# Key-page splits earlier in the sample attention, two memory projections behind the scores, and the last two selections spread over later heads

## The reference, cut to what matters

```
# sample request b: keys = 256 cached + 8 new, the best 66 by an indexer score are kept
sc  = where(key_pos <= q_pos, indexer_scores(qi, iw, ki_all), -inf)
sel = top_k(sc, 66)
p   = softmax(q . k[sel] * HEAD_DIM**-0.5);  o = p . v[sel]          # 8 heads of 64

# prompt, in blocks of 128 queries (i = 0..7): keys 0..128*(i+1)-1, the best 256 are kept
sc  = where(key_pos <= q_pos, indexer_scores(qi, iw, ki), -inf)
sel = top_k(sc, 256)                                                # blocks i >= 2 have more than 256
o   = softmax(q . k[sel] * HEAD_DIM**-0.5) . v[sel]                 # per head

# memory: mk, mv = split(rms_norm(mem) @ w_kv), 256 rows x 2048 columns
```

## Time and profile before

| | before |
|---|---|
| three executions | 1844.61, 1849.56, 1849.82 us (median 1849.56) |
| the profiled execution | 1846.91 us, span 1845.1 us |
| mean granted TensorE clock | 0.96 |
| busy: PE | 1707.6 us (93%) |
| busy: VectorE (DVE) | 1114.9 us (60%) |
| busy: ScalarE (ACT) | 811.0 us (44%) |
| busy: GpSimd (POOL) | 733.7 us (40%) |
| the chain that ended last | PE 71%, DVE 15%, ACT 6%, issue 4%, POOL 2%, DMA 2% |
| sample attention | about 445 to 562 us of the span |
| prompt's attention | about 562 to 735 us |

### The profile page before, as it was taken

One profiled execution on the slowest core, in us unless ns is written; L12 is line 12 of the kernel. 1 busy time (PEld: TensorE's weight loads), 2 busy tenths in 40 slices (PEclk: granted clock), 3 DMA queues, 4 the chain that ended last, 5 costly groups with the idle time before them and its releaser, 6 DMA issues.

```text
span 1845.1 us, 33734 instructions
## 1 busy us (share of the span) xinstructions
PE 1707.6 (93%) x13725; PEld 1187.0 (64%) x13803; DVE 1114.9 (60%) x1902; ACT 811.0 (44%) x1476; POOL 733.7 (40%) x704
## 2 busy tenths in 40 slices
PE   6999999996776899989887997999999999999998
PEld 3544445444444655545577544888888888899898
DVE  5856656787797764456655238888788787300000
ACT  5455688655435764432456226435444444110100
POOL 3232365987341200320023426666666666411200
PEclk9999999998797999999988998999999999999999
DMA  7031112023522110301344112121121222321211
GB/s 231 9 109 55 35 45 83 23 81 108 168 90 89 62 38 10 103 1 35 106 154 131 58 52 81 47 70 47 49 68 47 62 54 86 98 95 40 95 38 27
DMA packets 136548, 132.75 MB, mean 72 GB/s; under 512 B 15358, under 2 KB 109630, under 8 KB 136356
## 3 DMA queue, kind: packets, MB, share of 16 engines
q1 hardware_dynamic: 123850, 118.79, 20.7%
q10 hardware_dynamic: 12544, 11.80, 2.0%
HBM read 114.58 MB, written 15.98 MB: 71 GB/s over the span
## 4 chain that ended last, share of the span: by engine, by line
PE 71%; DVE 15%; ACT 6%; issue 4%; POOL 2%; DMA 2%; SPq 0%; ACTq 0%; DVEq 0%; POOLq 0%
PE PS L1558 23%; PE PS L1615 5%; PE PS L1616 5%; PE PS L1617 5%; PE PS L940 4%; PE PS L941 4%; PE PS L942 4%; ACT arena L1631 2%; PE PS L1104 2%; PE PS L1102 2%; PE PS L1103 2%; PE PS L1260 2%; ACT arena L1690 2%; PE PS L1272 1%; POOL arena L2964 1%
## 5 line engine op out<-in xcount | busy, mean ns | idle before, releaser
L1558 PE MATMUL PS<-arena 128*128 128x272 f16 (+1 forms) x3696 | 430.5, 280 | 5.0 <-issue 5.0
L1558 PEld LDWEIGHTS PS<-arena 128*128 128x128 f16 (+1 forms) x3696 | 362.5, 98 | 73.1 <-issue 5.4
L1631 ACT ACTIVATE arena<-PS 128x512 f16<-128x512 f32 (+11 forms) x381 | 189.9, 529 | 235.1 <-PE PS L942 81.3
L1631 ACT ACTIVATE arena<-arena 128x512 f16<-128x512 f32 (+5 forms) x214 | 136.3, 658 | 238.6 <-PE PS L1558 117.1
L368 POOL TENSOR_TENSOR arena<-arena 128x512 bf16<-128x512 f32 (+2 forms) x144 | 161.8, 1158 | 184.1 <-ACT arena L359 183.8
L940 PE MATMUL PS<-arena 128*128 128x512 f16 (+3 forms) x648 | 228.1, 362 | 5.2 <-DVE arena L2597 1.4
L941 PE MATMUL PS<-arena 128*128 128x512 f16 (+3 forms) x648 | 227.5, 361 | 0.0
L1615 PE MATMUL PS<-arena 128*128 128x256 f16 (+1 forms) x792 | 216.0, 273 | 1.4 <-POOL arena L918 1.0
L1617 PE MATMUL PS<-arena 128*128 128x256 bf16 (+1 forms) x792 | 215.9, 273 | 0.0
L1616 PE MATMUL PS<-arena 128*128 128x256 f16 (+1 forms) x792 | 215.9, 273 | 0.0
L942 PE MATMUL PS<-arena 128*128 128x512 bf16 (+2 forms) x608 | 212.0, 359 | 0.0
(11 more groups left out here) (351 smaller groups left out, 3693.6 us busy)
## 6 DMA issues: line engine op xcount, KB each, us to landing
arena<-w_gu SPq DMA_DIRECT2D x44, 512.0 KB, 4.8
arena<-w_down SPq DMA_DIRECT2D x8, 1408.0 KB, 7.8
arena<-w_in SPq DMA_DIRECT2D x8, 1024.0 KB, 5.1
arena<-w_kv_mem SPq DMA_DIRECT2D x8, 1024.0 KB, 7.2
arena<-cache_mem_k SPq DMA_DIRECT2D x32, 256.0 KB, 3.4
arena<-cache_mem_v ACTq DMA_DIRECT2D x28, 256.0 KB, 3.9
arena<-w_in SPq DMA_DIRECT2D x24, 256.0 KB, 3.8
arena<-x_prompt SPq DMA_DIRECT2D x9, 512.0 KB, 6.3
```

Source lines behind the costliest of these rows:

```text
L1558: mm = e.matmul(PS[:, product_bank(f, i) + c, 0:TC], w[:, i, k], s[i][:, q, c, :], start=first, stop=last)
L1631: e.activation(out, in_, ACT.Copy, **kw).then_inc(sem(name), 1)
```

## The change

Four edits, each a move or a condition. No instruction is added or removed.

1. PE: parts 4 and 6 of the memory projection no longer do three groups ahead of the scores; now only the odd parts do, so the wait for a new chunk's weights stands behind the scores.
2. ScalarE: the copies of the next key pages (`page_out`) stand ahead of the weight split, the `sign_step` and the exponential.
3. VectorE: the low parts of the next key pages (`page_lo`) stand right behind the maximum, ahead of the selection's part or `update()` and of the normalisation.
4. VectorE: in the prompt's attention a part of the selection runs only if fewer than four blocks are done, or from head 23 on. Four are done when it begins, so the five open parts (B and C of block 3, A, B and C of block 2) move from heads 0 to 4 to heads 23 to 27.

```diff
+SELECT_FROM = 23
@@ PE, sample attention
-                    if part and part > 2:
+                    if part and part % 2:
                         memory_part(part, 0, 3)
...
                     if part:
-                        memory_part(part, 3 if part > 2 else 0, 6)
+                        memory_part(part, 3 if part % 2 else 0, 6)
@@ ScalarE, step b
                 if b == 5:
                     memory_roots()
+                if b + 1 < DEC_B:
+                    for pg in range(NPG):
+                        page_out(b + 1, pg)
                 if b == 0:
                     e.wait_ge(sem("s2_mm"), NI)
                     B.split_hi(e, 1)
...
                     e.activation(p_s[:, b % 2, :], PS[0:NS, b % 2, 0:PAST + NS], ACT.Exp, bias=sat_st[:, 1, b:b + 1],
                                  scale=ATT_SCALE, accum_out=sat_st[:, 2, b:b + 1]).then_inc(sem("sa_exp"), 1)
-                if b + 1 < DEC_B:
-                    for pg in range(NPG):
-                        page_out(b + 1, pg)
@@ VectorE, step b
                 e.tensor_scalar(sat_st[:, 1, b:b + 1], sat_st[:, 0, b:b + 1], -ATT_SCALE, None, ALU.mult
                                 ).then_inc(sem("sa_nm"), 1)
+                if b + 1 < DEC_B:
+                    page_lo(b + 1, 0)
+                    page_lo(b + 1, 1)
                 if updates[0] == BITS and b < DEC_B - 1:
                     turn(PARTS_SAMPLE[0])
                 update()
...
-                if b + 1 < DEC_B:
-                    page_lo(b + 1, 0)
-                    page_lo(b + 1, 1)
@@ VectorE, prompt's attention, head m
-                turn(PARTS_ATT)
+                if done[0] < 4 or m >= SELECT_FROM:
+                    turn(PARTS_ATT)
```

## The result

| | before | after |
|---|---|---|
| median (lowest to highest) | 1846.74 us (1844.18 to 1849.82, 11 runs) | 1852.04 us (1849.77 to 1853.58, 11 runs) |
| ratio, 95% interval | | 1.0028 (1.0018 to 1.0037) |
| the profiled execution | 1846.91 us | 1853.19 us |

The changed kernel is slower by 5.2 us, between 3.3 and 6.8. The forecast was +2.6 us with "no change" as the likeliest case, so the sign of the sum is right, and it is too small. All ratios here are of fast executions; one of e9's ten, of 4459.63 us, isn't among them.

The account below looks back on a forecast made before the run. PE was taken as busy 93% of the span, with VectorE's list the clock from 480.7 to 500.9 us. The terms +0.7 + 0 - 5.9 + 7.8 = +2.6 us on 1846.91 gave 1849.5 us, range 1840 to 1857.

Parts of the forecast that it names:

- What bounds the kernel: Sample and prompt attention: from 480.7 to 500.9 us VectorE's list is the clock, busy 19.47 of 20.20 us.
- Edits 2 and 3, steps 0 to 2: Sample attention, key pages moved earlier: a later weight load less page work saved on VectorE, +0.7 us.
- The second half of the split of chunk 2 waits for just this transfer: ScalarE, sample attention: this split waits only for the chunk 2 weight load, taken as 1.9 us late.
- The credit of 1.2 us: VectorE, steps 0 to 2: page work no longer stands behind the exponential, -1.2 us.
- the +1.9 for the late split: Steps 0 to 2: the chunk 2 load, and the split that waits for it, come 1.9 us later.
- Edits 2 and 3, steps 3 to 7: Sample attention: VectorE has the same operations in another order and hardly a wait, 0 us.
- Edit 1: PE, sample attention: scores come sooner but nobody needs them, and the projection product is taken out later, 0 us.
- Edit 4, heads 0 to 4: Prompt attention: five selection parts of 9.38 us leave VectorE's list, 3.5 us become waits for PE, -5.9 us.
- Edit 4, heads 23 to 27: Prompt attention: the deferred parts add 5.3 us to the loop and 2.5 us by meeting POOL, +7.8 us.
- Slack takes it all: Rival: deferred parts fall into VectorE's waits and chunk 2's load isn't late, -7.4 us, 1839.5 us; chance 0.18.
- Lock with POOL: Rival: in heads 24 to 26 each two-input VectorE operation waits for a POOL operation, +8.0 us, 1854.9 us; chance 0.16.

Follow-up runs that it names:

- e9: Kernel before with both key-page moves, but ScalarE's copies in step 0 left behind the exponential as before; ratio 1.0010.
- e7: Kernel before with both key-page moves, but in step 2 ScalarE's two page copies stand behind the split of weight chunk 2; ratio 1.0023.
- e5: Kernel before with only ScalarE's page copies moved ahead, VectorE's page subtractions left in place; ratio 1.0035.
- e6: Kernel before with only VectorE's page subtractions moved ahead, ScalarE's page copies left behind the exponential; ratio 1.0039.
- e11: Kernel before with both key-page moves, but VectorE's subtractions behind the search update or selection part, still ahead of the wait for the exponential; ratio 1.0040.
- e1: Kernel before with only the two key-page moves of ScalarE and VectorE, projection order and head loop unchanged; ratio 1.0039.
- e12: Kernel before with only the five selection parts moved, one each ahead of head 0 and at heads 1, 7, 23 and 37; ratio 0.9950.
- e3: Kernel before with only the selection parts moved, out of the first heads to heads 23, 29 and 33 to 35; ratio 0.9990.
- e4: Kernel before with the two key-page moves from step 3 on only, steps 0 to 2 as before; ratio 1.0030.
- e2: Kernel before with only the head-loop gate that defers five selection parts to head 23 and later; ratio 1.0009.

## Why the prediction was wrong in its verdict, point by point

- *What bounds the kernel.* Held. From 480.7 us on VectorE's list is the clock of the stage, and the losses of both kinds reached head 0 in full.
- *Edits 2 and 3, steps 0 to 2: +0.7 us.* **This step failed.** It measured +2.7 against the profiled execution of before, +2.1 against the mean of the six traces with the old code (46.65 us). The first half of its chain came out: split of chunk 1 forecast at 450.6 us (450.27), value pages not before 463.9 (462.50), the load late. What failed was "The second half of the split of chunk 2 waits for just this transfer": it was not asked what `page_out(3)`, moved ahead of that same split, waits for, though the same question had been put for `page_out(1)`. The trace shows 3.26 us of wait for PE there, and behind it PE's 7.00 us of wait for POOL's low halves of chunk 1 and 2.2 us more for the same products at the lower granted clock. The forecast followed these low halves to the value pages and the load, and not to PE. e7 shows that the load was late too, by 2.3 us to the first half, in the range that the text gave and above the 1.9 it took. The credit of 1.2 us for page work that no longer stands behind the exponential appeared in full (1.19); the term mis-sized is the +1.9 for the late split, which measured +3.7. e5 shows that ScalarE's move alone costs about 6 us there, and against it the changed kernel that VectorE's takes 3.5 off; by itself (e6) that one is worth nothing.
- *Edits 2 and 3, steps 3 to 7: 0 us.* **This failed too**, by 2.65 us. The text knew that POOL and VectorE slow one another and took the meetings as a matter of chance, "one or two either way". They are not: the value pages of POOL follow the exponential at a fixed distance, the subtractions push the scan back by 1.2 us in every step, and three of four scans meet POOL in the same way. e11 shows it.
- *Edit 1: 0 us.* Held (changed kernel against e1).
- *Edit 4, heads 0 to 4: -5.9 us.* It was -7.5. The mechanism held and the size was off; the wait for PE ahead of head 2 grew to 2.84 us as worked out, but PE's next scores came at 1.47 us instead of the 2.06 taken from the old loop, and the low part and copy behind them took 2.5 us instead of 3.3. Here is the chain of waits of the changed kernel:

```profile
572.47 2.76 PE PS L1261 x12
...
578.98 1.47 PE PS L1261 x12
```

- *Edit 4, heads 23 to 27: +7.8 us.* It was +7.6. The waits of 1.46 and 0.90 us are gone as forecast, the one of 3.17 shrank to 1.73, and one of 0.34 grew to 1.14. Contention is 1.6 us, not 2.5: parts of C that took 0.75 and 0.43 us at heads 0 to 4 take 1.52 and 1.26, and part A met none. So the sum of the two terms of edit 4, forecast at +1.9, came out at +0.1 (7.63 - 7.52), and the error of 1.6 us in heads 0 to 4 hid part of the loss that was missed: that the total is as near as +2.6 against +5.2 is partly luck. These are the two operations and the wait (VectorE, changed kernel):

```profile
639.86 1.52 DVE L2448 SCALAR_TENSOR_TENSOR arena<-arena 128x512 f16<-128x512 f32 x1
641.42 1.26 DVE L2450 TENSOR_SCALAR arena<-arena 128x512 f32<-128x512 f16 x1
...
653.57 0.69 DVE L2598 TENSOR_TENSOR arena<-PS,arena 128x512 bf16<-128x512 f32 x1 [1.14 <-ACT arena L1632]
```

- *The rivals.* "Slack takes it all" fell at each of its three points. "Lock with POOL" reached +8.0 by 13.2 us in heads 23 to 27; those took 7.6. A lock with POOL did bring half of the loss, but in steps 3 to 6, where no rival had put it. By the rule of the Trainium skill (page "SBUF — State Buffer", section "Who interferes with whom"), a VectorE operation with two SBUF inputs and a POOL operation that reads SBUF exclude each other, and the order of their starts decides which of them waits. The rows agree. Both engines get slower, POOL by 1.2 to 2.5 us a pair; the scan of step 3, which started 1.09 us ahead of POOL, kept its 2.29 us while POOL's pair took 4.87; and the scans of steps 4 to 6, which started 0.31, 0.25 and 0.17 us behind POOL, took 0.84 us more each, near to what was left of POOL's first subtraction (1.16 us alone).
- *What remains open.* The ratio is 1.0039 for e1 and 1.0028 for the changed kernel, though their traces are equal up to head 0 and the gate is worth about zero: the intervals overlap, and the difference wasn't taken further. Nor was it tried whether e12 and the good part of the moves (e9's steps 0 to 2 with e11's order from step 3 on) add up.

## What to carry to other kernels

When an operation is moved ahead of another in an engine's list, ask of every iteration what the moved operation itself waits for, and what the one behind it feeds. Here two copies in step 0 held back a 3.7 us split, and with it another engine's low halves, PE's next product, a queue and a load; the same edit without step 0 was a gain in that stretch. Deferred work was free in two kinds of place: in a wait of VectorE under another engine's long operation (ScalarE's weight splits), and where another engine was busy without a break (PE at heads 36 to 40). It was not free in idle time that is shared out over the steps of a loop in which no engine is full: 5.6 us at heads 33 to 35 cost 5.57 although VectorE had 1.8 us idle there, while of the 9.4 us that e12 spread over the other places 8.1 went from the heads' time (160.72 us from head 0 to 63 before, 152.60 in e12, 158.2 to 162.6 in the kernels with the old heads). And where an engine's neighbour repeats its work at a fixed distance in every step, contention is systematic and has to be priced per step.

## What the runs showed of the hardware

The code behind the attention is the same in all kernels, but its time isn't. Busy time by stretch, from one maximum of VectorE in the cross-attention (line 2645 of before, 2647 of the changed kernel) to the next, of before and of the changed kernel (start:end, length, busy us of PE, PE's weight loads, DVE, ACT, POOL, then the granted clock, DMA share and GB/s):

```profile
931.35:942.76 11.41, 8.81 (x144) 7.80 (x145) 6.71 (x12) 7.28 (x18) 4.04 (x5) 0.85 0.53 169
```

```profile
934.81:948.34 13.53, 10.93 (x144) 9.07 (x145) 6.71 (x12) 7.32 (x18) 5.71 (x6) 0.62 0.46 146
```

The same 144 matrix products take 10.93 us of PE instead of 8.81, at a granted clock of 0.62 against 0.85, and the stretch is longer by just that, 2.12 us. Up to the following such maximum (957.51 us in before, 963.67 in the changed kernel) the loss is 2.7 us. It is 2.4 to 3.3 us in all other traces but those of e3, e4 and e6, which have none of it. So it is not the change's own: e2 and e3 have the same code but for the place of five parts, and e2 has it and e3 not. Why the clock falls in the one and not in the other is not shown, nor is whether the spread of one kernel's runs (1844 to 1850 us before) comes from it, since one execution of each was profiled. So a difference of 3 us between two medians here can be more or less than what the edit does in its own stretch, and the stretches of the trace are the better measure of an edit, the medians of what it is worth.
